# Rows of a normalisation turned to features tile by tile, and the low parts of the expert input shared out anew over VectorE, ScalarE and GpSimd

## The reference

```python
z = x @ w_in                      # rnn stream, q, k, v, two gates
m = sigmoid(g_rnn) * (RGLRU(conv(z)) @ w_br_rnn) + sigmoid(g_attn) * (attention(z) @ w_br_attn)
x = LayerNorm(alpha * x + m @ w_out)                 # first normalisation of the layer
scores = sigmoid(x @ w_router)                       # 64 experts
# group-limited choice: 4 of 8 groups, then 8 experts for each token; gates = scores, normalised, * 2.5
ff = (silu(x @ ws1) * (x @ ws3)) @ ws2 + sum_e gate_e * (silu(x @ w1[e]) * (x @ w3[e])) @ w2[e]
x = LayerNorm(alpha * x + ff)                        # second normalisation of the layer
```

## Time and profile before

| | us |
|---|---|
| median of 3 runs | 1621.61 (1620.44 to 1621.72) |
| span of the profiled execution | 1618.9 |
| PE busy | 1577.1 (97%) |
| DVE busy | 749.1 (46%) |
| ACT busy | 570.5 (35%) |
| POOL busy | 23.0 (1%) |

### The profile page before, as it was taken

How to read it: one execution, slowest core, us unless ns; L and a number is a source line. 1 busy time by engine, 2 the same in 40 slices (tenths; PEclk the granted TensorE clock), 3 DMA queues, 4 the chain that set the end, 5 groups by cost and what they waited for, 6 DMA issues and landing times.

```text
span 1618.9 us, 25680 instructions
## 1 busy us (share of the span) xinstructions
PE 1577.1 (97%) x9514; PEld 1042.4 (64%) x9514; DVE 749.1 (46%) x1543; ACT 570.5 (35%) x1132; POOL 23.0 (1%) x38
## 2 busy tenths in 40 slices
PE   7999999999999999999999999999999999999997
PEld 6968997645555554555588699965555555455553
DVE  5668666234333323433574786562433332342336
ACT  4756443222232222223257664342223223222322
POOL 2000000000000000000010000000000000000000
PEclk9999999999999999999999999999999999999999
DMA  8552456499999999999436434458999999999990
GB/s 231 185 195 94 132 163 234 186 402 390 404 406 391 406 389 414 383 413 394 165 118 213 160 101 154 141 208 318 383 409 398 398 403 396 402 404 393 409 379 31
DMA packets 141556, 477.35 MB, mean 295 GB/s; under 512 B 10020, under 2 KB 74084, under 8 KB 108724
## 3 DMA queue, kind: packets, MB, share of 16 engines
q1 hardware_dynamic: 139728, 473.50, 75.8%
q0 software_dynamic: 1408, 2.85, 0.6%
q10 hardware_dynamic: 356, 0.13, 0.0%
HBM read 474.88 MB, written 1.57 MB: 294 GB/s over the span
## 4 chain that ended last, share of the span: by engine, by line
PE 93%; DVE 4%; ACT 1%; issue 1%; DMA 0%; SPq 0%; DVEq 0%; ACTq 0%
PE ps L881 27%; PE ps L901 14%; PE ps L556 7%; PE ps L569 6%; PE ps L570 6%; PE ps L571 6%; PE ps L922 4%; PE ps L863 4%; PE ps L923 4%; PE ps L864 4%; PE ps L866 2%; PE ps L910 1%; PE ps L843 1%; PE ps L889 1%; PE ps L665 1%
## 5 line engine op out<-in xcount | busy, mean ns | idle before, releaser
L881 PE MATMUL ps<-experts,xg 128*64 128x512 f32 x2048 | 450.5, 592 | 0.0
L881 PEld LDWEIGHTS ps<-experts,xg 128*64 128x64 f32 x2048 | 147.9, 137 | 290.6 <-issue 289.7
L901 PE MATMUL ps<-experts,hidT 128*64 128x512 f32 x1024 | 233.8, 598 | 1.1 <-ACT hidT L1247 1.1
L569 PE MATMUL ps<-parts 128*128 128x288 f32 x736 | 223.5, 304 | 2.4 <-DVE dense_lo L1375 2.1
L571 PE MATMUL ps<-parts,dense_lo 128*128 128x288 f32 x736 | 216.6, 294 | 0.0
L1703 DVE TENSOR_TENSOR hid<-ps,hid 128x256 f32<-128x256 f32 x64 | 27.2, 425 | 385.1 <-ACT hid L1241 385.1
L1255 ACT ACTIVATE yh<-ps,gsl 128x512 fp32r<-128x512 f32 x128 | 88.0, 687 | 230.1 <-PE ps L901 230.1
L1241 ACT ACTIVATE hid<-ps 128x256 f32<-128x256 f32 x64 | 24.6, 384 | 397.6 <-PE ps L881 397.6
L1715 DVE SCALAR_TENSOR_TENSOR yl<-ps,gsl,yh 128x512 fp32r<-128x512 f32 x128 | 96.1, 751 | 122.9 <-ACT yh L1255 122.9
L1233 ACT ACTIVATE xg<-ps,gperm_all 128x256 f32<-128x256 f32 x256 | 130.6, 561 | 61.4 <-PE ps L866 57.8
L901 PEld LDWEIGHTS ps<-experts,hidT 128*64 128x64 f32 x1024 | 68.2, 136 | 121.1 <-issue 121.1
(11 more groups left out here) (285 smaller groups left out, 2038.3 us busy)
## 6 DMA issues: line engine op xcount, KB each, us to landing
experts<-in_w SPq DMA_DIRECT2D x384, 1024.0 KB, 9.4
dense<-in_w_in SPq DMA_DIRECT2D x34, 1024.0 KB, 5.6
dense<-in_w_br_rnn SPq DMA_DIRECT2D x8, 1024.0 KB, 5.4
dense<-in_w_br_attn SPq DMA_DIRECT2D x8, 1024.0 KB, 5.1
dense<-in_w_out SPq DMA_DIRECT2D x8, 1024.0 KB, 5.2
dense<-in_ws SPq DMA_DIRECT2D x6, 1024.0 KB, 5.6
tok<-in_x_prompt SPq DMA_DIRECT2D x1, 1024.0 KB, 5.4
out_y_prompt<-tok SPq DMA_DIRECT2D x2, 512.0 KB, 2.6
```

The source lines that it names most:

```text
L569: mm(bank[:, 0:T], w_hi[:, k, col:col + P], hi[:, k, :], start=k == 0, stop=False)
L881: last = mm(ps[e % 2 * CAP:(e % 2 + 1) * CAP, 2, :], xg[:, k, e * CAP:e * CAP + CAP], experts[:, e, 0:2, k * DE:k * DE + DE], start=k == 0 ...
L901: last = mm(ps[e % 2 * CAP:(e % 2 + 1) * CAP, 3 + b, :], hidT[:, m, e % 2 * CAP:(e % 2 + 1) * CAP], experts[:, e, 2, m * D + b * 512:m * D ...
```

## The change

Seven edits:

1. `fill_normed` takes the place of `fill_xT` behind both normalisations. PE begins with four chunks of tile 0 when that tile stands, goes on with tile 1, and takes tile 2 last. Since a bank can be filled only when the token rows in it have been read, `FILL` is now 0 to 7 in order.
2. `keep_clock` is 4 products in place of 5, and 3 in place of 7. After the last layer there is none.
3. DVE no longer copies the high part of tile 0, nor makes the low part of tile 0 before `norm_back`. It makes the low parts of tiles 0 and 2 behind `one_hot`; that of tile 1 it does not make.
4. ACT makes all three high parts, behind the sigmoids.
5. GpSimd makes the low part of tile 1, when `xh_ready` counts two, with the features in another order of its loops.
6. GpSimd clears the padding of `xh[:, 2]`, earlier; the gather waits for its signal `pad_clear`.
7. Between the layers DVE runs `norm_back` before `low_parts`.

```diff
-FILL = (0, 1, 4, 5, 6, 7, 2, 3)
+FILL = tuple(range(KC))
...
                 pool.wait_ge(states_stored, (L + 1) * 64)
+                pool.wait_ge(br_used, (L + 1) * KC)
+                carry_wait(pool)
+                nc.gpsimd.memset(xh[2 * TS:P, NT - 1, :].bitcast(F32), 0.0).then_inc(pad_clear, 1)
+                pool.wait_ge(pad_clear, L + 1)
+                pool.wait_ge(xh_ready, L * NT + 2)
+                carry_wait(pool)
+                spread = lambda x: x.rearrange("p (k f) -> p f k", k=KC)
+                nc.gpsimd.tensor_tensor(spread(xl[:, 1, :]), tok[:, 1, :].rearrange("p (f k) -> p f k", k=KC),
+                                        spread(as_f(xh[:, 1, :])), ALU.subtract).then_inc(xl_ready, 1)
...
+            def fill_normed(L, k, first):
+                def turned(t, cs):
+                    at, n = TOK[t]
+                    for c in cs:
+                        last = transpose(ps[:, FILL[c], at:at + n], tok[0:n, t, c * P:c * P + P], ident[0:n, 0:n])
+                        if t == NT - 1:
+                            last.then_inc(z_ready[c % 2], 1)
+                for b in range(2):
+                    bank_of(L, first + b)
+                before = (2 * L + k) * NT
+                pe.wait_ge(tok_act, before + 1)
+                turned(0, range(4))
+                pe.wait_ge(tok_act, before + 2)
+                turned(1, range(4))
+                turned(0, (4, 5))
+                turned(1, (4, 5))
+                pe.wait_ge(tok_act, before + NT)
+                pe.wait_ge(tok_dve, 2 * L + k + 1)
+                turned(2, range(6))
+                for c in (6, 7):
+                    for t in range(NT):
+                        turned(t, (c,))
...
-                keep_clock(0, 5)
-                pe.wait_ge(tok_act, (2 * L + 1) * NT)
-                pe.wait_ge(tok_dve, 2 * L + 1)
-                fill_xT(lambda c: bank_of(L, Z_FILL1 + c))
+                keep_clock(0, 4)
+                fill_normed(L, 0, Z_FILL1)
...
                                 pe.wait_ge(xl_ready, (L + 1) * NT)
+                                pe.wait_ge(pad_clear, L + 1)
...
-                keep_clock(0, 7)
                 if L < depth - 1:
-                    pe.wait_ge(tok_act, (2 * L + 2) * NT)
-                    pe.wait_ge(tok_dve, 2 * L + 2)
-                    fill_xT(lambda c: bank_of(L, Z_FILL2 + c))
+                    keep_clock(0, 3)
+                    fill_normed(L, 1, Z_FILL2)
...
-                act.wait_ge(xh_ready, L * NT + 1)
-                keep_high(1)
                 act.wait_ge(logits, L + 1)
                 act.wait_ge(score_clear, L + 1)
...
-                keep_high(2)
+                for t in range(NT):
+                    keep_high(t)
...
-                V.memset(xh[2 * TS:P, NT - 1, :].bitcast(F32), 0.0)
...
-                dve.wait_ge(tok_act, 2 * L * NT + 1)
-                V.tensor_copy(xh[:, 0, :].rearrange("p (k f) -> p f k", k=KC),
-                              tok[:, 0, :].rearrange("p (f k) -> p f k", k=KC)).then_inc(xh_ready, 1)
-                keep_low(0)
                 norm_back(L, V_G1, V_B1, Z_FILL1)
...
-                keep_low(1)
...
                     if first:
+                        keep_low(0)
                         keep_low(2)
                         dve.wait_ge(xl_ready, (L + 1) * NT)
...
                 if L < depth - 1:
+                    norm_back(L, V_G2, V_B2, Z_FILL2)
                     low_parts(L + 1, 0)
-                if L < depth - 1:
-                    norm_back(L, V_G2, V_B2, Z_FILL2)
```

More of the change, by code:

```diff
@@ L372, in build @@
         next_round = sem("next_round")
+        pad_clear = sem("pad_clear")
         first_half_full = sem("first_half_full")
```

## The result

The changed kernel takes 1627.94 us (median of 4 runs, 1627.54 to 1629.33) against 1621.66 (1620.44 to 1622.26) for the kernel before: ratio 1.0037, 95% interval 1.0025 to 1.0048. It is slower, by some 6 us, where 1621.0 and no measurable change were forecast.

What follows compares the result with a forecast made beforehand. PE bounds the kernel (93% of the last-ending chain), so only its idle or filler time can be won. 1.9 - 1.05 - 0.25 = 0.6 us won, 1621.61 to 1621.0 us; range 1616.5 to 1624.3.

Steps and rivals of the forecast that it cites:

- The fill of the first normalisation: Layer 0 router: tile 2's transposes begin at 261.9, router products end at 265.4 instead of 268.03, 2.6 us won.
- The table load: ACT before the sigmoid: 1.28 us load now waits for `logits`, uncovered; sigmoid at 268.15, leaving 1.35 us won.
- GpSimd stops DVE: Choice of experts: POOL's 2.7 us subtraction from 272.9 holds L1655 2.4 us; layer 1 loses 1.05 us.
- The library row: Layer 0, ahead of POOL's subtraction: priced 1.28 us, so only L1664 is stopped, 1.6 us; 0.25 us lost.
- Between the layers: Fill before layer 1: tile 2 begins at 811.0 instead of 812.93, 1.9 us won.
- The time around the span: Whole run: 2.7 us between span and median, added to the forecast span of 1618.3.
- The clock: Rival, layer 1 ranks: PE idles some 3.7 us, half clock costs 4 us more, 1625.0; chance 0.05.
- the forecast's likeliest case: Choice of experts: POOL stops DVE with 1.8 to 3.5 us of work, 1619.2 to 1622.6; chance 0.45.

Runs made afterwards that it cites:

- last experiments: Changed kernel with tile 1's low part back on DVE and the sigmoid table loaded early: 1618.37 us, ratio 0.9976; with small filler products too, 1618.40 us.
- The first experiment: Changed kernel with 4 filler products of PE ahead of its wait for the choice of experts: 1625.15 us, ratio 1.0017.
- the two profiles with filler there: Changed kernel with 4 filler products before PE's wait for the choice, 1625.15 us; the same plus small filler in both fills' pauses, 1624.97 us.
- the fills alone: Kernel before with only `fill_normed`, `FILL` in order and the fewer filler products: 1623.69 us, ratio 1.0013.
- the small filler added: Kernel before with the new fills and 224-column filler products between tile 0's and tile 1's transposes: 1623.29 us, ratio 1.0010.

## Why the prediction was wrong

The time lies outside the range, on the slow side. Point by point:

- **The fill of the first normalisation: right.** The 8 chunks are through the router at 265.79 against 265.4 forecast and 268.03 before; 2.4 us won for 2.6, if the 0.12 that the changed kernel is late by on entry are left out. Tile 2's transposes do not stand at 261.9, since PE has to finish all 20 before the first product; they end at 263.7.
- **The table load: right.** It begins when L850 ends and is exposed in full. The sigmoid begins at 268.69 for 268.15 forecast, 0.8 us earlier than before for 1.35. PE's gain is that of the chain, as said: with the load back in the pause (last experiments) the ranks come 2.1 us earlier.
- **GpSimd stops DVE: right, and the size too.** 2.86 us for 2.7, L1681 2.29 us longer for 2.4, from 272.99 for 272.9. In layer 1 the choice cost 1.40 for 1.05. The operation that it met is L1681, which is L1653 before, and not L1655 as forecast, as the sigmoid came 0.54 us later than forecast.
- **The library row: wrong in its price.** It was taken as 1.28 us and left layer 0 with a loss of 0.25. The trace shows nothing between ACT's copy (to about 272.8) and the subtraction at 272.99, and in layer 1, without the row, the subtraction begins only 0.1 us sooner behind the start of ACT's copies: next to no price. So layer 0 has the stop of layer 1, and loses 1.47. The Trainium skill's GPSIMD Engine Reference, section 2.1, would have about 6 us for a first call of freshly loaded code; nothing like it is seen here, though the trace does not show whether the code was freshly loaded.
- **Between the layers: right in kind, 1.29 won for 1.9.** Tile 1 made PE wait 1.26 us, and the first product follows all 20 transposes, not the eight before tile 2.
- **The time around the span: taken wrongly.** The 2.7 us are in no run: it is 1.8 for the kernel before and 2.3 for the changed one. The forecast added the same to both, so the level of 1621.0 did not suffer, but 0.5 us of the 6.3 is a term that it did not have.
- **The clock: here the forecast failed.** It was named as a rival, at 0.05, and only for layer 1. The argument against it was that at 4.50 us busy in 6.00 the clock was 1.00. That row has PE's idle time in pieces, the longest 1.50 us; the forecast's own working gave one unbroken pause of 3.7. A row is evidence for its own kind of pause only. The clock fell in both layers, and the products behind the pauses cost 1.80 and 3.04 us, where the rival had 4 in one layer and the sum had nothing. That is the step that failed: the pause in front of the ranks was counted, the slow products behind it were put at no cost. The first experiment shows it: with the pause filled, those 4.6 us are gone, and the spans of the two profiles with filler there, 1620.7 and 1620.6 without the slow start, are what the forecast's likeliest case comes to with the other terms at their measured size (1618.9 + 3.0 - 1.3 = 1620.6).

The library row (1.2 us), the smaller gain between the layers (0.6) and layer 1 (0.35) would by themselves have given 1621.0 + 2.2 = 1623.2, in the range; the clock put the time outside.

What stays open is what decides whether the clock falls in a short pause. At the ranks pauses of 3.65 and 3.56 us brought it down, 2.80, 2.23 and 1.37 did not. But in the fills it fell behind 1.88 and not behind 1.76, and behind the same 0.36 and 1.26 in the profiles of two variants and not in those of the others that have these pauses. Whether the filler that the change leaves out is part of it was not tested by itself. How much a run lost can be estimated from its mean granted clock: the profiled execution that lost 4.8 us behind its pauses has 0.994, the three that lost 2.9 to 3.2 have 0.995, those that lost nothing have 0.996 or 0.997. (The runs of the kernel before have 0.998 or 0.999. The other kernels have no filler in the last 20 us of the span, where PE has almost no work left: the clock there reads 0.70 to 0.77, against 0.89.) By this most of the spread of the fills alone is the clock. A count of the runs under 0.996 points at one place: eight of ten with the fills alone and eleven of twelve with the small filler added, where PE stands 1.73 to 1.88 us for DVE inside the router products; none of 19 with the low part back on DVE, with or without the early table load, where that stop is absent and the pauses between the layers are the same. No run tests this by itself. Where each run lost it, only its profile would tell.

## What to carry to other kernels

Work moved to GpSimd was not off VectorE's path here, since both read SBUF: first ask which VectorE operation will be running then, and put the GpSimd instruction where that one has slack. An engine that wins time ahead of a chain that it must wait for only trades work for a pause; if that engine is PE, price the pause and the products behind it, and fill it when it is long. When a wait is deleted or moved, look at which instruction now carries it, a table load above all.

## What was not expected of the hardware

- The granted clock fell to 0.50 behind single pauses of 3.6 us, at a cost of 1.80 and 3.04 us, and four filler products (3.60 us) prevented it.
- The 32 first products of L568 took 8.00 us or 9.71 to 10.38 in the profiles of variants with the same code there, with the clock column at 1.00 both times.
- A stop by GpSimd is shown as a longer VectorE instruction and not as idle time: 2.43 us for 3 elements. An operation with one SBUF input and 24 elements took 0.74 us in place of 0.18, another of that size kept its 0.18.
- The row that selects GpSimd's library cost at most 0.1 us, and GpSimd's subtraction of 1024 elements a partition with strided inputs took 2.86 us, where DVE takes 1.94.
